# A thirteenth unit of the input projection by seven products, and new counts of filler between the mixers' steps

## What is computed

```python
for l in range(DEPTH):                       # DEPTH = 2
    h = rms_norm(x, norm_mix_pre[l])
    z = h @ w_in[l]                          # the input projection, 1024 -> 6144
    q_h, f_fw, f_bw, i_h, g_h, q_d, k_d, v_d, gate_a, gate_b = jnp.split(z, splits, axis=-1)
    a = hgrn2_mixer(q_h, f_fw, f_bw, i_h, g_h, lb[l], hgrn_gnorm[l])      # 4 heads, gated scan both ways
    b = diff_attention(q_d, k_d, v_d, diff_lambda[l], ...)                # 4 heads
    m = sigmoid(gate_a) * (a @ w_branch_a[l]) + sigmoid(gate_b) * (b @ w_branch_b[l])
    x = x + rms_norm(m @ w_out[l], norm_mix_post[l])
    x = x + rms_norm(conv_ffn(rms_norm(x, norm_ffn_pre[l]), ...), norm_ffn_post[l])
    x = x + rms_norm(sigmoid(rms_unit(x) @ w_ple_gate[l]) * (p[l] @ w_ple[l]), norm_ple[l])
```

## Time and profile before

| | us |
|---|---|
| three runs | 2409.86, 2410.37, 2410.99 (median 2410.37) |
| the profiled execution | 2410.16 |
| its span | 2408.2 |
| TensorE busy | 2398.9 (100%) |
| VectorE busy | 1837.6 (76%) |
| ScalarE busy | 1311.3 (54%) |
| GpSimd busy | 196.8 (8%) |
| granted TensorE clock | 1.00 in every slice (2.4 GHz) |

### The profile page before, as it was taken

The page is one execution under the profiler, slowest core; times in us unless marked ns, Lnnn a source line. Parts: engine busy times, 40 slices in busy tenths (PEclk is TensorE's granted clock), DMA queues, the critical chain, the costliest instruction groups (busy, mean ns, idle before and its releaser), DMA issues.

```text
span 2408.2 us, 40381 instructions
## 1 busy us (share of the span) xinstructions
PE 2398.9 (100%) x16184; PEld 2240.6 (93%) x16184; DVE 1837.6 (76%) x2412; ACT 1311.3 (54%) x2023; POOL 196.8 (8%) x236
## 2 busy tenths in 40 slices
PE   9999999999999999999999999999999999999998
PEld 8999999998999999888889999999989999998887
DVE  7656788764888899978585568886649889999784
ACT  6445666542555556456454456665436555564563
POOL 1001011100200000003110011111001000000031
PEclk9999999999999999999999999999999999999999
DMA  5354444354222233733234544434433133346421
GB/s 185 129 175 141 137 148 134 126 182 145 92 90 90 84 97 129 282 128 118 97 131 131 185 136 141 141 128 155 159 137 110 60 96 95 102 165 238 162 88 62
DMA packets 284673, 320.97 MB, mean 133 GB/s; under 512 B 10436, under 2 KB 216776, under 8 KB 284488
## 3 DMA queue, kind: packets, MB, share of 16 engines
q1 hardware_dynamic: 211680, 171.39, 22.8%
q10 hardware_dynamic: 72808, 147.01, 16.9%
HBM read 253.08 MB, written 65.27 MB: 132 GB/s over the span
## 4 chain that ended last, share of the span: by engine, by line
PE 99%; DVE 0%; ACT 0%; issue 0%; DVEq 0%; POOLq 0%; POOL 0%; ACTq 0%
PE ps L909 23%; PE ps L1192 15%; PE ps L1397 13%; PE ps L1137 11%; PE ps L882 6%; PE ps L1503 5%; PE ps L1120 3%; PE ps L1366 3%; PE ps L1333 3%; PE ps L896 3%; PE ps L1252 3%; PE ps L1089 2%; PE ps L1109 1%; PE ps L1018 1%; PE ps L961 1%; PE ps L1483 1%
## 5 line engine op out<-in xcount | busy, mean ns | idle before, releaser
L2149 DVE TENSOR_TENSOR wlo<-raw,whi 128x1024 fp32r<-128x1024 f32 (+1 forms) x152 | 163.9, 1079 | 55.0 <-ACT whi L3177 55.0
L909 PE MATMUL ps<-hT_hi,whi 128*128 128x384 f32 x608 | 203.1, 334 | 0.0
L909 PE MATMUL ps<-hT_hi,wlo 128*128 128x384 f32 x608 | 203.1, 334 | 0.0
L909 PE MATMUL ps<-hT_lo,whi 128*128 128x384 f32 x608 | 203.1, 334 | 0.0
L3191 ACT ACTIVATE U<-ps 128x384 f32<-128x384 f32 x152 | 74.8, 492 | 223.9 <-PE ps L909 223.9
L1397 PE MATMUL ps<-whi,PH_hi 128*128 128x512 f32 x456 | 179.0, 393 | 0.4 <-issue 0.4
L1397 PE MATMUL ps<-whi,PH_lo 128*128 128x512 f32 x456 | 177.7, 390 | 0.0
L1397 PE MATMUL ps<-wlo,PH_hi 128*128 128x512 f32 x456 | 177.5, 389 | 0.0
L1711 DVE TENSOR_TENSOR wlo<-raw,whi 128x1024 fp32r<-128x1024 f32 (+1 forms) x98 | 102.8, 1069 | 80.2 <-ACT whi L2645 80.0
L1584 DVE TENSOR_TENSOR wlo<-raw,whi 128x2048 fp32r<-128x2048 f32 x53 | 121.2, 2286 | 50.7 <-ACT whi L2469 50.7
L909 PE MATMUL ps<-S_hi,whi 128*128 128x384 f32 x456 | 152.3, 334 | 0.0
(11 more groups left out here) (349 smaller groups left out, 6938.5 us busy)
## 6 DMA issues: line engine op xcount, KB each, us to landing
raw<-w_up_dram SPq DMA_DIRECT2D x88, 512.0 KB
raw<-w_in_dram SPq DMA_DIRECT2D x62, 512.0 KB
raw<-w_down_dram SPq DMA_DIRECT2D x60, 512.0 KB, 4.6
raw<-w_in_dram SPq DMA_DIRECT2D x16, 1024.0 KB
zT<-gst ACTq DMA_DIRECT2D x40, 384.0 KB, 2.5
GT<-zT ACTq DMA_DIRECT2D x16, 768.0 KB, 5.9
pD<-CG ACTq DMA_DIRECT2D x26, 384.0 KB, 2.3
zT<-hn ACTq DMA_DIRECT2D x48, 192.0 KB, 1.9
```

The costliest lines, as they stand in the source:

```text
L909: ins = mm(ps[:, 4 * (j % 2) + bank, 0:TH], quarter(L, W[y], j, (w,))[:, 0, k * P:(k + 1) * P], sum_operand(a, x, k), start=(opens and k = ...
L2149: v.tensor_tensor(lo, x, hi.bitcast(F32), ALU.subtract)\
```

## The change

Gate unit 0 becomes unit 14 and is done by the seven half-size products (now 13 units, `I1` = 15); its weights are loaded in the arrangement of such a unit. The plain unit ahead of the mixers is gone: both token units, (2, token) and (3, token), are filler units 15 and 16, and gate units 1 to 7 are units 17 to 23. With 9 filler units as before there are 72 parts, now counted 20, 17, 18 and 17 for the four heads: head 0 has two parts in slot 0, heads 1 and 3 one part instead of two in slot 3. The first part of heads 1, 2, 3 is number 20, 37, 55 instead of 18, 36, 54.

The first head's rope is done beside units 12 and 13, silu, silu gate and the attention splits beside units 13 and 14; the queries come behind the first maxima on DVE; on ACT `merge_keys` comes ahead of the first exponentials; on PE the first scores stand right behind the last product, then slot 0, then the diagonal, which waits for the last unit's copies. GpSimd's totals wait for product P3 of unit 14. The splits of slot 0 move into level 0 on DVE. SP issues the loads for head 3's attention one unit earlier. The weight buffers' turn and the places of quarters in them no longer shift from layer to layer.

```diff
-IN_UNITS = [(0, TOKEN_U), (1, TOKEN_U)] + [(h, u) for h in range(NH) for u in range(3)] + [(2, TOKEN_U), (3, TOKEN_U)]\
-    + [(None, u) for u in range(2 * NH)]
+IN_UNITS = [(0, TOKEN_U), (1, TOKEN_U)] + [(h, u) for h in range(NH) for u in range(3)] + [(None, 0)]\
+    + [(2, TOKEN_U), (3, TOKEN_U)] + [(None, u) for u in range(1, 2 * NH)]
-I0, I1 = 2, 14
+I0, I1 = 2, 15
-SLOTS = ((0, 2, 2, 2, 2, 2, 2, 1, 1, 0, 2, 1, 1), (0, 2, 2, 2, 2, 2, 2, 1, 1, 0, 1, 2, 1),
-         (0, 2, 2, 2, 2, 2, 2, 1, 1, 0, 2, 1, 1), (0, 2, 2, 2, 2, 2, 2, 1, 1, 0, 1, 2, 1))
+SLOTS = ((2, 2, 2, 2, 2, 2, 2, 1, 1, 0, 2, 1, 1), (0, 2, 2, 1, 2, 2, 2, 1, 1, 0, 1, 2, 1),
+         (0, 2, 2, 2, 2, 2, 2, 1, 1, 0, 2, 1, 1), (0, 2, 2, 1, 2, 2, 2, 1, 1, 0, 1, 2, 1))
...
+                    elif h is None and j < I1:
+                        load(unit(L, j), [rows(w_in, L, 0, KD, 8 * HW + u * 256 + b * P, P) for b in range(2)])
...
-                        if j == min(DENSE + (first - 2) // 8 + (2 if head == 2 else 3), N_IN - 1):
+                        if j == min(DENSE + (first - 2) // 8 + 2, N_IN - 1):
                             load_qk(L, head)
...
# PE, mixers and ahead of them
+                side(PRE)
                 if h == 0:
+                    pe.wait_ge(in_act.sem, in_act.at(L, f"c21_{I1 - 1}"))
+                    pe.wait_ge(in_dve.sem, in_dve.at(L, f"c12_{I1 - 1}"))
                     gla_diagonal(it)
-                side(PRE)
...
-                for p in range(8):
-                    if p == 4:
-                        pe.wait_ge(in_act.sem, in_act.at(L, f"c21_{I1 - 1}"))
-                        pe.wait_ge(in_dve.sem, in_dve.at(L, f"c12_{I1 - 1}"))
-                        att_scores(L * NH, 0)
-                    project(unit(L, I1), p, True, ((0, 7), (6, 6)))
-
+                att_scores(L * NH, 0)
...
# DVE
                     att_max(it, 0)
-                    low(unit(L, DENSE))
+                    gla_queries(it)
                     att_weights(it, 0)
-                side(PRE)
...
-                    if k == 0 and h:
-                        for t in range(TAIL, len(SLOTS[h - 1])):
+                    if k == 0:
+                        side(PRE)
+                        for t in range(TAIL, len(SLOTS[h - 1])) if h else ():
                             for j in side_splits(h - 1, t):
                                 low(unit(L, j))
-                    elif k:
+                    else:
                         side(k)
...
+                        att_low(L * NH)
                         low(unit(L, I1))
-                        for n in ("cqk", "sqk", "radd"):
-                            att_rope(L * NH, L, n)
...
+                    for n in {I1 - 3: ("cqk", "sqk"), I1 - 2: ("radd",)}.get(e, ()):
+                        att_rope(L * NH, L, n)
...
-                att_low(L * NH)
-                gla_queries(L * NH)
...
# POOL
+                g.wait_ge(in_pe.sem, in_pe.at(L, f"P3{I1 - 1}"))
                 gla_totals(L * NH)
...
# ACT
+                    if not more:
+                        gla_silu(L * NH)
                     in_copy(L, e, "u2")
...
+                        gla_silu_gate(L * NH)
                         done(in_pe, L, f"P2{e}")
                         high(unit(L, I1))
                     in_store_first(L, e)
                     in_copy(L, e, "u3")
+                    if e == I1 - 2:
+                        att_high(L * NH)
...
-                gla_silu(L * NH)
-                gla_silu_gate(L * NH)
                 gla_sigmoids(L * NH)
                 gla_sigmoid_neg(L * NH)
                 in_copy(L, I1 - 1, "c21")
                 in_store_rest(L, I1 - 1)
                 load_v(L, 0)
-                att_high(L * NH)
-                high(unit(L, I1 + 1))
-                copy_out(L, I1, 0, (0, 7))
-                store_out(L, I1, 0)
-                att_exponentials(L * NH, 0)
                 done(lay_dve, L, "slw")
                 merge_keys(L * NH, 0)
-                copy_out(L, I1, 1, (6, 7))
+                att_exponentials(L * NH, 0)
```

More of the change, by code:

```diff
@@ L560, in unit @@
             n, half = L * N_UNITS + j, L * ((U_DN + N_UNITS - U_PG) // 2) + (j - (U_PG - U_DN if j >= U_PG else 0)) // 2
-            turn = (j + L + (j >= U_PG)) % 2
+            turn = (j + (j >= I1) + (j >= U_PG)) % 2
             return (n, half, j % 2, turn) if i is None else (n + i * each, half + i * (each // 2), j % 2, turn)
@@ L580, in in_quarter @@
         def in_quarter(L, w, e, names):
-            at = [((PLACE[k] + (e % 2 if k == "B22" else 0)) + 4 * L) % 8 * 512 for k in names]
+            at = [(PLACE[k] + (e % 2 if k == "B22" else 0)) * 512 for k in names]
             return view(w[:], at[0], [[at[-1] - at[0] or 512, len(at)], [1, 512]])
@@ L625, in ring_at @@
         def ring_at(L, n):
-            return (n + 2 * (L + 1)) % 4 * 1024
+            return n % 4 * 1024
         def ring(L, w, n):
@@ L637, in quarter @@
         def quarter(L, w, j, names):
-            at = [((PLACE[k] + (j % 2 if k == "B22" else 0)) + 4 * (L + 1)) % 8 * 512 for k in names]
+            at = [(PLACE[k] + (j % 2 if k == "B22" else 0)) * 512 for k in names]
             return view(w[:], at[0], [[at[-1] - at[0] or 512, len(at)], [1, 512]])
@@ L2751, in mixers @@
                     gla_diagonal(it)
-                    store_out(L, I1, 1)
                 side(PRE)
```

## The result

The changed kernel takes 2434.67 us (median of four, 2434.03 to 2435.30) against 2410.14 before: the ratio is 1.0101, with an interval of 1.0084 to 1.0119. It is slower by 24.5 us. The forecast was 2439.0, range 2423 to 2450.

The account below looks back on a forecast made before the run. TensorE (PE), busy 2398.9 of 2408.2 us, was taken as the bound. Per layer, 11.8 for copy waits + 3.5 for other slot effects + 1.1 entry - 2.1 saved = +14.4, twice +28.8: 2439.0 us, range 2423 to 2450.

Parts of the forecast that it names:

- The eight sizes: Eight half-unit boundaries, six inside slots: PE waits for ACT's copy out of banks 6 and 7; 11.8 us a layer.
- slot 11 to 12 of head 1: Boundary with only transposes between: about 0.5 us if ACT is free, 2.3 behind the weights' copy; 1.7 taken.
- The second slot of head 2: Boundary inside the slot: PE at 378.83 waits for ACT, whose queued work ends at 379.94, then the copy; 1.98 us.
- What else the slots move: Thin third levels of heads 1 and 3 (1.45), far keys in tails of head 2 (1.5) and head 0 (0.6); 3.5 a layer.
- The entry: Before head 0's second scores, a DVE and ACT chain of 8.2 against 7.1 of PE work: 1.1 us stall, bounds 0 and 3.
- The saving: Gate unit as seven products, 84 matmuls instead of 96: 12 fewer a layer, 2.1 us, possibly 2.9.
- Covered after all: Rival: ACT copies early at all eight places, levels and entry lose nothing, only the saving remains; 2406.0 us, 4%.
- hand-overs hidden: Rival: no cost at the eight boundaries, the rest as worked out; +2.5 a layer, 2415.2 us, 5%.
- The short form: Rival: each of eight boundaries costs only copy and restart, about 1.0, as ACT's queue clears sooner; +7.4 a layer, 2425, 15%.
- Stalls stack: Rival: later copies delay ACT's exponentials, so scores and weights transposes come late; 3 to 6 us more a layer, 2445 to 2452, 13%.
- The clock falls: Rival: new PE gaps drop the clock to 1.2 GHz in parts of the mixers; over 2450 us, 3%.
- Not what it says: Rival: first head's preparation cannot start before the last product, so PE waits; up to 8 us a layer, 2455, 3%.

Follow-up runs that it names:

- experiment 1: Kernel before with only head 1's filler counts changed (slot 3 one part, slot 10 two), putting three half-unit boundaries inside slots: 2420.35 us, ratio 1.0043.
- experiment 2: Changed kernel with filler counts 20, 18, 18, 16, so each half unit ends with a slot; no filler in the last head's slot 11: 2420.30 us.
- second version of experiment 6: Changed kernel with 20, 16, 18, 18 parts, no half unit ending inside a slot, and first head's maxima and exponentials early: 2409.09 us, ratio 0.9995.
- experiment 3: Changed kernel with ACT's copy of a half unit that ends inside a slot issued in that slot, ahead of ACT's other work there: 2430.97 us.
- experiment 5: Changed kernel with the far keys' input on DVE ahead of the next head's second rope product: 2434.83 us, ratio 1.0103.
- experiment 7: Second version of experiment 6 with far keys' input and output scaling earlier on DVE: 2407.97 us; beside it, same order with 18 parts per head: 2409.09.
- experiment 4: Changed kernel with the first head's maxima ahead of its keys on DVE and its exponentials ahead of merge_keys on ACT: 2433.49 us, ratio 1.0095.

## Why the prediction was right, point by point

- **Direction and mechanism.** The hand-over of banks 6 and 7 was named as the main cost, at the eight right places. Experiments 1 and 2 show it from both sides: put into the kernel before, it costs what it should, and with the counts changed it is gone.
- **The eight sizes.** Forecast 11.8 a layer, measured 9.3. In the order of the prediction's list: 1.14 (1.26 forecast), 1.35 (1.98), 1.15 (1.27), 1.60 (1.72), 1.69 (1.80), 1.27 (1.38), 0.61 (0.73), 0.50 (1.7). Six are right within 0.2, all of them too high by 0.11 or 0.12. PE runs again 0.05 after the copy's end, where 0.15 was put: that is most of it.
- **The term that was mis-sized most** is slot 11 to 12 of head 1. I took 1.7 between bounds of 0.5 and 2.3, on the ground that the weights' copy of 1.92 and DMA issues were queued on ACT; in the trace of before that copy ends 0.33 after the end of slot 11. What I missed is that the new counts move this copy too: it goes with a unit's part 1, which is part 33, and that stood in slot 11 and now stands in slot 10. In the changed kernel it starts at 366.47 and is done 1.8 before the half ends, and ACT even idles for 0.22 ahead of the half's copy. The lower bound was the answer, 0.50.
- **The second slot of head 2** was 0.6 too high. ACT's copy of the transposed weights came 0.22 after PE reached the second part, where it had been 0.73 after the earlier trace rows. The likely reason is that an earlier stall of PE let ACT catch up, as the prediction allowed; this was only argued, no run has that stall alone.
- **What else the slots move.** Third levels 0.44, and 0.44 + 0.35 in head 3, against 0.5 and 0.95; far keys of head 2 1.50 against 1.5, of head 0 0.59 against 0.6. Together 3.3 against 3.5.
- **The entry.** It is 0.82 against 1.1, and the chain is as written: 5.25 to the end of the maxima (5.65), 7.87 to the scores (8.2). The 5.95 for 48 token matmuls is right too (5.94 in the trace), though 48 x 0.12, as it is written there, is 5.76. Behind each of the 30 table loads of the changed kernel ACT's next instruction starts within 0.02. The Trainium skill, ScalarE: Activation LUTs, section "What ACT_TABLE_LOAD costs", gives some 1380 ns of drain on top of every switch; the forecast of this stall would have been 2.5 by that (estimate), and the trace does not agree.
- **The saving.** 2.1 a layer was put, from 12 matmuls, and it is 2.0. The products cost 14.7 for 84 matmuls, 0.175 each. The second version of experiment 6 has mixers 15.2 shorter than before (254.39 against 269.58) with 1.5 of stalls left in them, so without stalls they would be 16.7 shorter.
- **The sum.** In the changed kernel the stalls (13.5) and what the starts behind them and waits too small for a row add (0.9) make 14.4 a layer, and less 2.0 that is +12.4, twice 24.8; the measured difference of the medians is 24.5. The forecast had 28.8, 4 too high. Over two layers 2.4 too much was put at slot 11 to 12 of head 1, 1.3 at the second slot of head 2, and 2.5 in small amounts at the other places. The 1.8 that the slower starts and small waits cost were not in the sum at all, and offset part of that. So the total is nearer than its largest terms are.
- **PE's busy time** was to fall by about 4 us, and it rose by 2.4. This sign of the prediction failed, while the matmuls did go (24 fewer, some 4.2 us). A row's busy time runs to the modelled end of the last matmul, so every stall adds some 0.1 to 0.2 to it, and the slower starts add more; with 28 stalls in two layers this is about the size of the difference (estimate).
- **The rivals.** *Covered after all* and *hand-overs hidden*: no, each hand-over costs at least 1.07 where PE asks at once (experiment 3). *The short form*, 1.0 each and 2425, described the floor of the six in-slot hand-overs nearly right (1.07), and their mean is 1.37, so ACT's queue is real: experiment 3 took 3.7 us off by removing it at five of them. Over all eight, though, the measured 9.3 lies nearer to its 8 than to the forecast's 11.8. Its 2425 came as low because its sum puts 2.3 for the other steps where the prediction has 4.6, without a reason; with 4.6 and a saving of 2.1 it gives 10.5 a layer, 2431.2, which is inside the forecast's own range. The two were never as far apart as their times. *Stalls stack*: no, the values products behind were not late. *The clock falls*: not in the changed kernel, whose longest wait is 1.5, but in experiment 2 behind one of 3.08. *Not what it says*: the first head was prepared beside the last products.

## What to carry to other kernels

When filler is cut into pieces that share an accumulator, count where its boundaries fall before changing any count: a boundary inside a slot costs the whole copy out of PSUM (here 1.07 us, up to 0.6 for what its engine has queued, and 0.13 of slower starts), one that falls between slots costs nothing where the bounding engine's work behind it outlasts the copy (behind two short pieces it cost 0.6 and 0.5), and a shift by one part moves all later ones. Moving work off the bounding engine makes every step it covered thinner; where a wait is then removed by reordering, see whether the other engine's whole list up to the next meeting point got shorter, or the wait will only move there (experiment 5 against 7). Here a saving of 4 us came with some 27 us of waits. With the counts and the orders of experiments 4 and 7 changed, 2.3 us of it are left.

## What the runs showed of the hardware

- The granted clock fell to 0.50 (1.2 GHz) behind an idle time of PE of 3.08 us in layer 0 of experiment 2, and came back 3.4 us later; behind an equal gap in layer 1 it stayed at 1.00, and the 30 waits of PE of up to 1.5 us in the changed kernel never moved it. So the price of the gap was 3.25 us in one case and about 4.6 in the other. This version's times also spread more than the others' (2418.98 to 2421.86), and its longest execution lists the lowest mean clock, 0.997, where the profiled one lists 0.999; that it holds more such falls is likely, but only the profiled one has a trace. The Trainium skill, TensorE: Matmul & The Clock Gate, section "A second HAM failure mode: psum-queue depth-cycling", tells of micro-idles between groups of matmuls that made the clock swing; with eight pauses of 0.5 to 1.7 us a layer at PSUM hand-overs, no row here shows that.
- PE takes up work 0.05 us after the end of the ACT copy that it waits for, at all 16 hand-overs of the changed kernel (the first: copy 339.32 + 0.82 = 340.14, first matmul at 340.19):

```profile
339.32 0.82 ACT L2596 ACTIVATE hn<-ps 128x768 f32<-128x768 f32 x1
```
